# A hybrid decoder step on one core: the depthwise convolution's last channel chunk computed by GpSimd alone, in another place of the program

## The reference

```python
z = rms_norm(x) @ w_in                      # q, k, v, gate_a, qi, ki, wi, glu_a, glu_b, gate_c
score[t, s] = sum_h wi[t, h] * relu(qi[t, h] . ki[s] / 8)      # indexer
idx = top_k(causal(score), 256)             # the 256 best keys of each query
attn = softmax(q . k[idx] / 8 + rel_bias) @ v[idx]
u = glu_a * sigmoid(glu_b)                  # 512 channels
c[t, ch] = dw_b[ch] + sum_j dw_w[j, ch] * u[t - 30 + j, ch]    # depthwise, 31 taps
conv = silu(layer_norm(c))
y = x + concat(attn * silu(gate_a), conv * silu(gate_c)) @ w_out
```

## Time and profile before

| | |
|---|---|
| median of 3 runs | 1131.39 us |
| the runs | 1131.02, 1131.39, 1137.29 us |
| span of the profiled execution | 1135.0 us |
| PE, DVE, ACT, POOL busy | 1006.0, 763.8, 397.1, 198.9 us |
| granted TensorE clock, mean | 0.942 |

### The profile page before, as it was taken

One profiled execution on the slowest core, in us unless ns is written; L12 is line 12 of the kernel. 1 busy time (PEld: TensorE's weight loads), 2 busy tenths in 40 slices (PEclk: granted clock), 3 DMA queues, 4 the chain that ended last, 5 costly groups with the idle time before them and its releaser, 6 DMA issues.

```text
span 1135.0 us, 11359 instructions
## 1 busy us (share of the span) xinstructions
PE 1006.0 (89%) x3762; PEld 554.1 (49%) x3762; DVE 763.8 (67%) x1762; ACT 397.1 (35%) x811; POOL 198.9 (18%) x185
## 2 busy tenths in 40 slices
PE   3999998196899999999979996965898899999998
PEld 2866665063243443446433353534554654775443
DVE  5208979999896988879998889765567543441000
ACT  5311443132666546555400011226342432552000
POOL 0201699360450000000000000002023123000000
PEclk9899999598999999999989898986899999999999
DMA  7450020020663002020030000022023112000221
GB/s 270 147 179 0 1 74 2 1 75 1 216 214 108 28 37 85 0 74 1 0 103 18 19 18 1 1 106 106 19 80 97 30 55 67 1 1 12 74 75 65
DMA packets 35355, 69.88 MB, mean 62 GB/s; under 512 B 9633, under 2 KB 11977, under 8 KB 35289
## 3 DMA queue, kind: packets, MB, share of 16 engines
q1 hardware_dynamic: 28129, 43.99, 11.3%
q0 software_dynamic: 7168, 25.17, 7.0%
HBM read 58.50 MB, written 11.12 MB: 61 GB/s over the span
## 4 chain that ended last, share of the span: by engine, by line
PE 57%; DVE 27%; issue 5%; DMA 5%; ACT 3%; POOL 2%; SPq 0%; POOLq 0%; DVEq 0%; ACTq 0%
PE ps L489 53%; DVE ctmp L1306 11%; PE ps L492 4%; DMA KVr<-in_cache_k,idx 3%; DVE eqm L1372 2%; DVE junk L1372 2%; POOL ctmp L1799 2%; DMA KVr<-in_cache_v,idx 1%; DVE ct L1284 1%; DMA xn<-in_x_prompt 1%; DVE pv L1508 1%; DVE LB L1509 0%; ACT uT L1153 0%; POOL qz L1855 0%; ACT relu L1085 0%
## 5 line engine op out<-in xcount | busy, mean ns | idle before, releaser
L489 PE MATMUL ps<-W,xT 128*128 128x512 f32 (+3 forms) x720 | 279.0, 547 | 2.4 <-ACT gcT L923 1.2
L489 PE MATMUL ps<-xT,W 128*128 128x344 f32 x768 | 230.8, 463 | 0.0
L489 PEld LDWEIGHTS ps<-W,xT 128*128 128x128 f32 (+1 forms) x720 | 121.2, 185 | 152.9 <-issue 150.4
L489 PEld LDWEIGHTS ps<-xT,W 128*128 128x128 f32 x768 | 148.7, 195 | 79.7 <-issue 7.7
L1306 DVE SCALAR_TENSOR_TENSOR ctmp<-uT,chw,ctmp 128x1024 f32<-128x1024 f32 x90 | 172.4, 1916 | 3.1
L1121 ACT ACTIVATE sgj<-SC,candn 128x1024 bf16<-128x1024 f32 (+2 forms) x96 | 88.6, 924 | 43.2 <-DVE candn L1388 43.2
L489 PE MATMUL ps<-kT,qz 128*128 128x512 f32 (+3 forms) x192 | 80.7, 533 | 21.5 <-POOL qz L1855 11.5
L1799 POOL TENSOR_TENSOR ctmp<-ctmp,product 128x1024 f32<-128x1024 f32 x30 | 91.6, 3055 | 29.3 <-ACT product L1013 26.3
L489 PE MATMUL ps<-V,PTs 128*128 128x64 f32 x576 | 74.5, 276 | 11.9 <-ACT PTs L923 7.8
L923 ACT ACTIVATE PTs<-ps 128x512 f32<-128x512 f32 (+3 forms) x96 | 43.4, 486 | 118.6 <-PE ps L492 118.5
L1740 DVE TENSOR_TENSOR ps<-ps,TP 128x256 f32<-128x256 f32 (+1 forms) x64 | 26.5, 414 | 85.8 <-PE ps L489 83.5
(11 more groups left out here) (315 smaller groups left out, 1213.4 us busy)
## 6 DMA issues: line engine op xcount, KB each, us to landing
W<-in_w_in SPq DMA_DIRECT2D x8, 2048.0 KB, 8.7
xn<-in_x_prompt SPq DMA_DIRECT2D x8, 512.0 KB, 8.3
W<-in_w_out SPq DMA_DIRECT2D x1, 4096.0 KB, 12.9
GA<-in_x_prompt SPq DMA_DIRECT2D x16, 256.0 KB
out<-GA SPq DMA_DIRECT2D x16, 256.0 KB
out<-V SPq DMA_DIRECT2D x8, 256.0 KB
out<-zN SPq DMA_DIRECT2D x8, 256.0 KB
bias_rows<-tprow SPq DMA_DIRECT2D x1, 1536.0 KB, 9.9
```

The source lines that it names most:

```text
L489: return nc.tensor.matmul(out, lhsT, rhs, start=start, stop=stop)
```

## The change

- GpSimd alone computes the last chunk (3): `tensor_scalar` makes a product, `tensor_tensor` adds it to a new accumulator `pacc`. These 61 instructions stand in its queue behind the last causal mask, ahead of the wait for `masks_done`.
- VectorE does chunks 0, 1 and 2, again 93 instructions; the last tap of each writes straight into `conv`, and waits for the last-rows transposes.
- ScalarE's `products` and `chunk_copy` are gone.
- `product` and `pacc` lie in the space of `kT`. GpSimd waits for `ct_used` before it writes there, and ScalarE waits for GpSimd's last addition before it writes the first `kT` tile.
- TensorE waits for `taps_done` and `product_added` in place of `chunk_out`.

```diff
-    ctmp = sb("ctmp", [P, 3, SEQ], F32, rGC)
+    ctmp = sb("ctmp", [P, 2, SEQ], F32, rGC)
-    product = sb("product", [P, 2, SEQ], F32, rV)
+    product = sb("product", [P, 2, SEQ], F32, rQK + 18432)
+    pacc = sb("pacc", [P, SEQ], F32, rQK + 26624)
...
-    DVE_CHUNKS = [0, 2, 3]
-    POOL_CHUNK = 1
-    SLOT = {0: 0, 2: 1, 3: 0, 1: 2}
+    DVE_CHUNKS = [0, 1, 2]
+    POOL_CHUNK = 3
...
             if n == 11:
-                wait(chunk_out, 4)
+                wait(taps_done, NTAP)
+                wait(product_added, CW)
...
-        chunk_copy(0)
...
-            if j == 3:
-                chunk_copy(2)
-            if j == 8:
-                chunk_copy(1)
             piece_out("qi", m, qiT[:, m // 3, a:a + n], sx, ACT.Copy)
-            products(2)
...
-            if n == 3:
-                chunk_copy(3)
...
+                if n == 0:
+                    act.wait_ge(product_added, CW)
...
-                if m == 2 * CW:
-                    v.wait_ge(chunk_out, 1)
                 src = uT[:, c, j:j + SEQ]
-                acc_ = ctmp[:, SLOT[c], :]
+                acc_ = ctmp[:, m // CW % 2, :]
...
                     v.wait_ge(taps_done, m)
-                    ins = vec.scalar_tensor_tensor(acc_, src, chw[:, c, j:j + 1], acc_, ALU.mult, ALU.add)
+                    if j == CW - 1:
+                        if c < 3:
+                            v.wait_ge(last_rows_read, c + 1)
...
+                    ins = vec.scalar_tensor_tensor(conv[:, c, :] if j == CW - 1 else acc_, src, chw[:, c, j:j + 1], acc_, ALU.mult, ALU.add)
...
-            if m in (6, 9):
-                add_taps(6)
...
-            if m >= 6:
-                add_taps(1)
-        add_taps(CW)
...
+        c = POOL_CHUNK
+        g.wait_ge(ct_used, 32)
+        g.wait_ge(*plan.drained("chw"))
+        for j in range(CW):
+            src = uT[:, c, j:j + SEQ]
+            if j == 0:
+                pool.tensor_scalar(pacc[:, :], src, chw[:, c, 0:1], chw[:, c, CW:CW + 1], ALU.mult, ALU.add).then_inc(product_added, 1)
+                continue
+            if j >= 3:
+                g.wait_ge(product_added, j - 1)
+            pool.tensor_scalar(product[:, j % 2, :], src, chw[:, c, j:j + 1], 0.0, ALU.mult, ALU.add).then_inc(product_ready, 1)
+            g.wait_ge(product_ready, j)
+            g.wait_ge(product_added, j)
+            if j == CW - 1:
+                g.wait_ge(*plan.full("cp"))
+            pool.tensor_tensor(conv[:, c, :] if j == CW - 1 else pacc[:, :], pacc[:, :], product[:, j % 2, :], ALU.add).then_inc(product_added, 1)
```

More of the change, by code:

```diff
@@ L399, in build @@
     taps_done = sem("taps_done")
-    chunk_out = sem("conv_chunk_out")
     chain_s = sem("dve_chain")
@@ L972, in sample_row @@
             nc.scalar.activation(ss[0:NB, 15:16], ss[0:NB, 14:15], ACT.Copy).then_inc(srow_done, 1)
[L974 to L984, removed]
         def piece_out(g, m, dst, sdst, func):
@@ L993, in piece_out @@
             copy(dst, pt(tag)[:, 0:n], tag, func=func)
[L995 to L1014, removed]
         for c in range(4):
@@ L1019, in _ @@
                 piece_out("glub", m, uT[:, c, CW - 1 + a:CW - 1 + a + n], sT[:, 0], ACT.Sigmoid)
-                if c >= 2:
-                    products(2)
             for m in range(3 * c, 3 * c + 3):
@@ L1026, in _ @@
                 piece_out("glua", m, glua_r[:, m % 2, 0:n], sT[:, 1], ACT.Copy)
-                if c >= 2:
-                    products(1)
-        chunk_copy(0)
         for j, m in enumerate(QI_PIECES):
@@ L1305, in taps @@
                     v.wait_ge(taps_done, m)
-                    ins = vec.scalar_tensor_tensor(acc_, src, chw[:, c, j:j + 1], acc_, ALU.mult, ALU.add)
+                    if j == CW - 1:
+                        if c < 3:
+                            v.wait_ge(last_rows_read, c + 1)
+                        else:
+                            v.wait_ge(*plan.full("cp"))
+                    ins = vec.scalar_tensor_tensor(conv[:, c, :] if j == CW - 1 else acc_, src, chw[:, c, j:j + 1], acc_, ALU.mult, ALU.add)
                 ins.then_inc(taps_done, 1)
```

## The result

The changed kernel takes 1147.37 us in the median of its runs (1143.56, 1144.01, 1150.73 and 1162.33), the kernel before beside it 1131.2. The ratio, formed without a disturbed run (1162.33), is 1.0127 with a 95% interval of 1.0084 to 1.0169: slower by 10 to 19 us, where +18 and 1149 us were forecast.

What follows compares the result with a forecast made beforehand. The chain of waits was put 57% on TensorE and 27% on VectorE, whose taps take turns with GpSimd. Early part -39, search +65 and -8 gave +18, hence 1149 us; range 1091 to 1171, 8 times in 10.

Steps and rivals of the forecast that it cites:

- The early part: Before the scores: without GpSimd's additions beside VectorE's taps, the accumulation of scores begins 38.0 us earlier, at 241.5.
- The score stage: Between the first accumulation of scores and the search: `chunk_copy(3)` goes from ScalarE, taken as 1.0 us saved.
- Everything else there stays: In the score stage: apart from `chunk_copy(3)` nothing changes; the cached keys' gathers wait for VectorE before and after.
- The search: In the search: small VectorE instructions wait for GpSimd, +65 us, and TensorE holds the rounds back less, -8.
- TensorE's holding: In the search: of the 9.5 us by which TensorE's tiles hold back the rounds, 1.5 stay, so -8.
- In that gap two small ones pass: At a search round's end: two small VectorE instructions pass in 0.34 us free; the third waits for a whole GpSimd instruction.
- its sentence by the Trainium skill: In the search: two more copies of the round's tail take turns, making nine, a round of about 13 us and +25.
- The counts undisturbed: In the search: VectorE's counts, 1.00 us for 768 elements, are not slowed by GpSimd.
- After the search: Behind the search: what follows is chained to its end, and nothing there is touched.
- small instructions slip in: Rival, in the search: small instructions don't queue behind GpSimd, so only the early -39 counts; 1092 us, chance 0.18.
- The milder one: Rival, in the search: only the five two-input instructions take turns, or the product takes 0.95 us; about 1137 us, chance 0.22.
- Strict turns: Rival, in the search: GpSimd gets the port after every small instruction, or its product is long; 1170 us, chance 0.12.

Runs made afterwards that it cites:

- best version: Changed kernel with the search's small operands in PSUM and nine of the last twelve taps moved ahead of VectorE's wait for `sn`: 1089.63 us, ratio 0.9654.
- The added wait: Changed kernel with each GpSimd product also waiting for the addition just before it, which it doesn't need: 1139.47 us, ratio 1.0052.
- write-only run: Changed kernel with GpSimd's 61 instructions replaced by 62 memsets, so chunk 3 isn't computed: 1115.89 us in a single run.
- the kernel with two inputs only: Changed kernel with the search's small operands in PSUM, except `cand` and `c2`, which stay in SBUF: 1108.54 us, ratio 0.9792.
- the PSUM runs: Search's small operands moved to PSUM: in the changed kernel 1096.59 us, with `cand` and `c2` left in SBUF 1108.54, in the kernel before 1133.08.
- the kernel cut in halves: Changed kernel with each of GpSimd's 61 search instructions cut into two of 512 elements: 1165.72 us, ratio 1.0301.

## Why the prediction was right, step by step

- **The early part, -38.0.** Measured -40.2, and 1.8 of the 2.2 beyond the forecast were there at the first tap (87.90 for 89.72). Its cause was the one named: silencing the shared chunk gives it alone (1094.5 us), moving the chunk copies alone gives nothing (1133.1).
- **The score stage, -1.** Wrong in sign: it took 94.8 us in place of 92.3. The step "Everything else there stays" failed. Two of VectorE's transposes wait 1.6 and 1.9 us for TensorE (0.52 and 0.45 before), whose mean clock was 0.84 in that stretch (239.3 to 260), part of it at the lower of its two levels, where it was 1.00 in the same one before. This is no chance of one run. All nine kernels whose accumulation starts at 238 to 242 have a clock of 0.75 to 0.84 there, a stage of 94.8 to 96.2 us, and at its start a wait of TensorE of 3.32 us, while VectorE ends its last twelve taps. The three that start at 279 to 280, and the best version below 236, are without that wait and at 1.00, with 92.3 to 93.6 us. That the wait is what lowers the clock, no run tests by itself. With this stage the search began 37.6 us earlier, for a forecast of 39.
- **The search, +65 - 8 = +57.** Measured 241.1 - 188.7 = +52.4, out of terms that were off in opposite directions. GpSimd's product was sized at 1.5 us and takes 1.12, and the pauses are shorter (0.08 behind a product, none behind an addition), so its work is 107 us and not 127. The round beside it was to be 11.4 us and is 13.4 on average, 14.13 once settled, so that eight rounds pass and not eleven: 107.2 - 8 x 5.6 = 62.4 lost. The shorter work alone would have made +54.5 of the +65, and the longer rounds put 7.9 on it: that the term came out near its figure is luck. TensorE's holding fell by 10, not 8. The failing step is "In that gap two small ones pass", the gap of 0.34 us: behind an addition there is no pause, the next product doesn't wait for it. The added wait, which makes one, brings the round to 10.95, near the forecast's. The other part of it is that the first copy of the round's tail takes turns as well, which the sum left out and only its sentence by the Trainium skill counted, with a round of about 13.
- **The counts undisturbed.** Right: 1.00 us for 768 elements beside GpSimd, in every kernel, but for two of the write-only run (1.43 and 1.55), whose records begin while the `candn` ahead of them is still waiting.
- **After the search, 0.** 15 us arrive there by the profile, and by the ratio, 1.0127, it is 14.4 us.
- **The rivals.** That small instructions slip in is refuted by the six waits. The milder one is refuted by `bit` and `candn` in the changed kernel's rows and by the kernel with two inputs only: one-input instructions wait too. Strict turns is nearest to the mechanism behind an addition, the forecast's two at a time to that behind a product.

The Trainium skill (SBUF — State Buffer, Who interferes with whom) has the forms right that share with GpSimd: the accumulating count doesn't, two SBUF inputs do against a reader and not against a writer, `tensor_scalar` and copy in their two-port modes do against both. The write-only run and the PSUM runs agree with it, but for the copy of one element, which never waited. By its sentence whoever issues first has the shared ports for the whole instruction, and the other is fully blocked. That gives the waits of the changed kernel, and not those of the kernel cut in halves: a copy that takes 0.18 us alone took 26.25 there, through some 27 GpSimd instructions.

What stays open is how the turn is given at a boundary without a pause. In the changed kernel VectorE got in behind additions without one. In the halves every wait from the third round up to the last additions ended behind a pair of additions or between the two products, where a product came next; in the first two rounds two ended elsewhere. And the copy of 26.25 us let six places behind a pair of additions go by. No run separates the causes.

## What to carry to other kernels

Before work goes to GpSimd "while VectorE counts", look at the small instructions between the counts: each one that reads two SBUF operands, or copies or scales from SBUF to SBUF, can wait for a whole GpSimd instruction, and a dependent chain with nine of them, six of which waited, cost 8.5 us a round here. Put one operand of each into PSUM, and the two engines run side by side. Where that can't be done, try pauses in a long row of GpSimd instructions: they helped in both kernels that got them here.

## What the runs showed that I had not expected

- Shorter GpSimd instructions made it worse: a ratio of 1.0301 to the kernel before, against 1.0127. With a wait between all of them, 0.9985.
- A needless wait in GpSimd's queue won some 8 us: 1.0052 against 1.0127.
- A copy of a single element a partition (0.15 us) never waited, though it goes from SBUF to SBUF; one of 32 elements did.
- Starting the scores 40 us earlier made them 2.5 to 4 us longer, in every kernel where TensorE waited 3.32 us at their start.
